# Second mixer's values with high and low parts in one stationary tile, four buffers in the norms, last modulation sums moved to a norm

## What is computed

```python
def hybrid_mixer(h, w_in, b_f, g_q, g_k, w_o):
    proj = h @ w_in
    ...
    sb_out = stick_breaking_attention(split_heads(sb_q, N_SB_HEADS), ...)
    fq = rms_norm(split_heads(fox_q, N_FOX_HEADS), g_q[None, :, None, :])
    fk = rms_norm(split_heads(fox_k, N_FOX_HEADS), g_k[None, :, None, :])
    ...
    fox_out = forgetting_attention(fq, fk, split_heads(fox_v, N_FOX_HEADS), log_f_cum)
    heads = jnp.concatenate([sb_out, fox_out], axis=1)
    return heads.transpose(0, 2, 1, 3).reshape(b, s, MIX_WIDTH) @ w_o

def second_block(x, c, ...):
    c_act = jax.nn.silu(c)
    mod = c_act @ w_mod[l] + b_mod[l]
    sh1, sc1, ga1, sh2, sc2, ga2, sh3, sc3, ga3 = jnp.split(mod, N_MOD, axis=-1)
    h = modulate(rms_norm(x, g_ffn1[l]), sh1, sc1)
    x = x + 0.5 * (1 + ga1[:, None, :]) * swiglu(h, ...)
    h = modulate(rms_norm(x, g_mix[l]), sh2, sc2)
    x = x + (1 + ga2[:, None, :]) * hybrid_mixer(h, ...)
    h = modulate(rms_norm(x, g_ffn2[l]), sh3, sc3)
    x = x + 0.5 * (1 + ga3[:, None, :]) * swiglu(h, ...)
```

## Time and profile before

| | us |
|---|---|
| median of 3 runs | 1822.4 (1821.92 to 1823.87) |
| the profiled execution | 1822.21 |
| its span, first to last instruction | 1820.5 |
| PE busy | 1805.6 (99%) |
| PEld busy | 1500.7 (82%) |
| DVE busy | 974.6 (54%) |
| ACT busy | 663.7 (36%) |
| POOL busy | 30.7 (2%) |

### The profile page before, as it was taken

The page is one execution under the profiler, slowest core; times in us unless marked ns, Lnnn a source line. Parts: engine busy times, 40 slices in busy tenths (PEclk is TensorE's granted clock), DMA queues, the critical chain, the costliest instruction groups (busy, mean ns, idle before and its releaser), DMA issues. The chain is left out here.

```text
span 1820.5 us, 20752 instructions
## 1 busy us (share of the span) xinstructions
PE 1805.6 (99%) x8593; PEld 1500.7 (82%) x8593; DVE 974.6 (54%) x1349; ACT 663.7 (36%) x1020; POOL 30.7 (2%) x62
## 2 busy tenths in 40 slices
PE   9999999999999999999999999999999999999998
PEld 8888888887888888878888888888888888888887
DVE  5655453457777766674433333666757543333332
ACT  5544441334323323352222222564656432122222
POOL 0000000000000000000000000010100000000001
PEclk9999999999999999999999999999999999999999
DMA  5232233355586565233333332322121333333333
GB/s 151 74 88 82 81 87 90 90 184 172 188 257 228 186 199 193 82 94 103 93 91 94 94 103 84 91 58 58 47 58 36 93 93 101 96 93 104 93 90 96
DMA packets 321859, 200.02 MB, mean 110 GB/s; under 512 B 6712, under 2 KB 311270, under 8 KB 321766
## 3 DMA queue, kind: packets, MB, share of 16 engines
q1 hardware_dynamic: 320882, 196.31, 35.9%
q0 software_dynamic: 640, 2.10, 0.4%
q10 hardware_dynamic: 244, 0.30, 0.1%
HBM read 196.58 MB, written 2.10 MB: 109 GB/s over the span
## 5 line engine op out<-in xcount | busy, mean ns | idle before, releaser
L1466 PE MATMUL ps<-u_hi,w_hi 128*128 128x512 f32 (+1 forms) x1704 | 667.1, 391 | 3.3 <-ACT u_hi L471 1.1
L1466 PE MATMUL ps<-u_hi,w_lo 128*128 128x512 f32 (+1 forms) x1704 | 660.2, 387 | 0.0
L1466 PE MATMUL ps<-u_lo,w_hi 128*128 128x512 f32 (+1 forms) x1704 | 655.4, 388 | 0.0
L885 DVE TENSOR_TENSOR w_lo<-w_raw,w_hi 128x1024 fp32r<-128x1024 f32 (+2 forms) x307 | 364.3, 1187 | 269.6 <-ACT w_hi L451 268.6
L451 ACT ACTIVATE w_hi<-w_raw 128x1024 fp32r<-128x1024 f32 (+2 forms) x307 | 314.5, 1025 | 239.0 <-DMA w_raw<-in_w_down 79.7
L1466 PEld LDWEIGHTS ps<-u_hi,w_hi 128*128 128x128 f32 x1704 | 320.0, 188 | 71.7 <-issue 4.3
L1466 PEld LDWEIGHTS ps<-u_hi,w_lo 128*128 128x128 f32 x1704 | 319.9, 188 | 66.2
L1466 PEld LDWEIGHTS ps<-u_lo,w_hi 128*128 128x128 f32 x1704 | 318.8, 188 | 67.2 <-DVE u_lo L919 2.9
L1466 PE MATMUL ps<-y_hi,w_hi 128*128 128x512 f32 x656 | 256.0, 390 | 0.0
L1466 PE MATMUL ps<-y_hi,w_lo 128*128 128x512 f32 x656 | 255.3, 389 | 0.0
L1466 PE MATMUL ps<-y_lo,w_hi 128*128 128x512 f32 x656 | 255.2, 389 | 0.0
(11 more groups left out here) (279 smaller groups left out, 1299.8 us busy)
## 6 DMA issues: line engine op xcount, KB each, us to landing
mod_raw<-in_w_mod SPq DMA_DIRECT2D x72, 512.0 KB, 4.8
w_raw<-in_w_in SPq DMA_DIRECT2D x71, 512.0 KB, 3.9
w_raw<-in_w_ffn_up SPq DMA_DIRECT2D x44, 512.0 KB, 4.0
w_raw<-in_w_gate SPq DMA_DIRECT2D x44, 512.0 KB, 3.8
w_raw<-in_w_up SPq DMA_DIRECT2D x44, 512.0 KB, 3.8
w_raw<-in_w_down SPq DMA_DIRECT2D x32, 512.0 KB, 3.9
w_raw<-in_w_ffn_down SPq DMA_DIRECT2D x16, 512.0 KB, 4.1
w_raw<-in_w_down SPq DMA_DIRECT2D x16, 384.0 KB, 3.4
```

Of the source, the lines that this page charges most:

```text
L885: e.tensor_tensor(w_lo[u % SLOTS][:, 0:n_k, :], w_raw[u % SLOTS][:, 0:n_k, :], f32(w_hi[u % SLOTS][:, 0:n_k, :]), ALU.subtract).then_inc(l ...
L1466: return e.matmul(out_, lhsT, rhs, start=start, stop=stop, skip_group_check=skip)
```

## The change

**Values.** In the second mixer the low parts of the values go into the half of `v_hi` that held zeros: the tile of head `n` is its high part in its own 64 columns and its low part in the other 64. Two matmuls (with the high and with the low part of the probabilities) replace three; the result has high x (high + low) in the head's own rows of PSUM and low x (high + low) in the other rows. The heads can therefore no longer share a bank: the second head of a step writes the projection bank from which the next step's keys were taken (`value_bank`), and waits until it is read. ACT copies the low half across to the head's own rows of `pair_out` (`take_low`), DVE adds the high half (`add_high`). `at_out` now comes with the first head's sum and a new semaphore `second_out` with the second's; PE waits for `second_out` behind the scores of the next step, ahead of its first strip. The pairs 6 and 7 are summed in `t_b` and then cut like the others, pair 6 ahead of 4 and 5. POOL's two memsets go.

**Norms.** Four buffers instead of two (`t_b[0]`, `t_a[0]`, `t_b[1]`, `t_a[1]`), so that chunk `c` waits for the low part of chunk `c - 4`. In ffn1, DVE waits for `plain_total` one chunk later, and ACT waits for six low parts before it writes the root of the first block's last norm into `t_a[0]`.

**Modulation.** Group 2 has 24 tiles, group 3 has 16. Group 3 is turned by PE behind the sums of norm mix2, in the place of 12 of 18 filler matmuls, and reduced by DVE behind that norm.

```diff
-MOD_GROUPS = ((0, 20), (20, 32), (32, 52), (52, 72))
+MOD_GROUPS = ((0, 20), (20, 32), (32, 56), (56, 72))
...
+        def scaled_tile(c):
+            return (t_b[c // 2 % 2][:, :], t_a[c // 2 % 2][:, 2:2 + SEQ])[c % 2]
+        def own_rows(n):
+            return slice(HEAD_DIM * n, HEAD_DIM * (n + 1))
+        def value_bank(i, n):
+            if n == 0:
+                return bank(slot_banks(i, 0)[0])
+            return ubank(U["proj"] + 3 * i + 4) if i + 1 < N_STEPS else bank(slot_banks(i, 0)[2])
+        def pair_out(i):
+            return heads[:, i, :] if i < N_STEPS - 2 else t_b[i - (N_STEPS - 2)][:, :]
...
+            def take_low(i):
+                for n in range(2):
+                    e.wait_ge(at_valued, 2 * i + n + 1)
+                    e.activation(pair_out(i)[own_rows(n)], value_bank(i, n)[own_rows(1 - n)], ACT.Copy).then_inc(low_out, 1)
             def fill_head(c):
-                e.activation(u_hi[:, c, :], heads[:, c, :], ACT.Copy).then_inc(u_hi_set, 1)
+                e.wait_ge(second_out, c + 1)
+                e.activation(u_hi[:, c, :], pair_out(c), ACT.Copy).then_inc(u_hi_set, 1)
...
-                for c in range(2, KC):
-                    e.wait_ge(u_lo_set, f * KC + c - 1)
+                scaled(2)
+                low(1).then_inc(u_lo_set, 1)
+                for c in range(3, KC):
+                    if c >= 4:
+                        e.wait_ge(u_lo_set, f * KC + c - 3)
                     scaled(c)
                     low(c - 1).then_inc(u_lo_set, 1)
...
-                    ins = e.tensor_tensor(v_lo[:, :, h, cols], ubank(u)..., f32(v_hi[:, :, h, cols]), ALU.subtract)
+                    ins = e.tensor_tensor(v_hi[:, :, h, own_rows(1 - h)], ubank(u)..., f32(v_hi[:, :, h, cols]), ALU.subtract)
...
+            def add_high(i):
+                for n in range(2):
+                    e.wait_ge(low_out, 2 * i + n + 1)
+                    out_ = pair_out(i)[own_rows(n)]
+                    e.tensor_tensor(out_, value_bank(i, n)[own_rows(n)], out_, ALU.add).then_inc((at_out, second_out)[n], 1)
...
             total("mix2")
-            keep_busy(18)
+            mod_turn(3)
+            keep_busy(6, 0)
...
+                if n and i + 1 < N_STEPS:
+                    u_k = p0 + 3 * i + 4
+                    e.wait_ge(bank_read[u_k % 2], u_k // 2 + 1)
...
-                    ins = three(ps[:, slot_banks(i, 0)[0], j * P:SEQ], (v_hi[:, j, n, :], v_lo[:, j, n, :]), (p_hi[n][:, at], p_lo[n][:, at]),
-                                n == 0 and j == 0, True, skip=True)
+                    for pp in (p_hi[n], p_lo[n]):
+                        ins = mm(value_bank(i, n)[:, j * P:], v_hi[:, j, n, :], pp[:, at], j == 0 and pp is p_hi[n], True, skip=True)
...
                 (sb_scores if i < N_SB else fox_scores)(i)
+                if i:
+                    e.wait_ge(second_out, i)
```

More of the change, by code:

```diff
@@ L470, in norm @@
                     e.wait_ge(normed, n0 + h + 1)
-                    ins = e.activation(u_hi[:, 0, half(h)], t_b[0][:, half(h)], ACT.Identity, bias=shift(0))
+                    ins = e.activation(u_hi[:, 0, half(h)], scaled_tile(0)[:, half(h)], ACT.Identity, bias=shift(0))
                     ins.then_inc(first_half_hi if h == 0 else u_hi_set, 1)
@@ L474, in norm @@
                     e.wait_ge(normed, n0 + c + 2)
-                    e.activation(u_hi[:, c, :], t_b[c % 2][:, :], ACT.Identity, bias=shift(c)).then_inc(u_hi_set, 1)
+                    e.activation(u_hi[:, c, :], scaled_tile(c), ACT.Identity, bias=shift(c)).then_inc(u_hi_set, 1)
             def residual(u0, which=None):
@@ L672, in scalar @@
             e.wait_ge(plain_total, 1)
+            e.wait_ge(u_lo_set, FILL["ffn1"] * KC + 6)
             after_own(e.activation(plain_r, bank(5), ACT.Ln, bias=EPS_COL[EPS1], scale=1.0 / D_MODEL))
@@ L781, in scalar @@
             take_v(0)
-            e.wait_ge(pool_set, 10)
+            e.wait_ge(mod_turned, sum(MOD_BANKS))
             stage_v(0)
@@ L812, in scalar @@
                     stage_normed(0)
-                e.wait_ge(at_valued, 2 * i + 2)
-                e.activation(heads[:, i, :], bank(slot_banks(i, 0)[0]), ACT.Copy).then_inc(at_out, 1)
+                take_low(i)
                 stage_v(i + 1)
@@ L831, in scalar @@
                     cut_hi(u + 3)
-                    e.wait_ge(at_valued, 2 * i + 2)
-                    e.activation(u_hi[:, i, :], bank(slot_banks(i, 0)[0]), ACT.Copy).then_inc(u_hi_set, 1)
+                    take_low(i)
+                    fill_head(i)
                     break
@@ L846, in scalar @@
                         fill_head(c)
-                e.wait_ge(at_valued, 2 * i + 2)
-                if i + 2 == N_STEPS:
-                    e.activation(u_hi[:, i, :], bank(slot_banks(i, 0)[0]), ACT.Copy).then_inc(u_hi_set, 1)
-                else:
-                    e.activation(heads[:, i, :], bank(slot_banks(i, 0)[0]), ACT.Copy).then_inc(at_out, 1)
+                take_low(i)
                 stage_v(i + 1)
                 if i + 2 == N_STEPS:
-                    for c in HEAD_ORDER[5:7]:
+                    for c in HEAD_ORDER[4:7]:
                         fill_head(c)
@@ L928, in norm @@
                     scaled(0, half(h))
-                if which == "ffn1":
-                    e.wait_ge(plain_total, 1)
                 scaled(1)
@@ L1252, in vector @@
             norm("mix2", U["gate_f"])
+            for k in range(MOD_BANKS[3]):
+                mod_sum(3, k)
+            mod_finish(3)
             p0 = U["proj"]
@@ L1340, in fill_head @@
                 e.wait_ge(u_hi_set, FILL["heads"] * KC + pos + 1)
-                e.tensor_tensor(u_lo[:, c, :], heads[:, c, :], f32(u_hi[:, c, :]), ALU.subtract).then_inc(u_lo_set, 1)
+                e.tensor_tensor(u_lo[:, c, :], pair_out(c), f32(u_hi[:, c, :]), ALU.subtract).then_inc(u_lo_set, 1)
             cut_lo(p0 + 2)
@@ L1380, in vector @@
                     stage_normed(i + 1)
+                add_high(i)
                 stage_v(i + 1)
@@ L1395, in vector @@
                     cut_lo(u + 3)
-                    e.wait_ge(u_hi_set, FILL["heads"] * KC + KC)
-                    e.tensor_tensor(u_lo[:, i, :], bank(slot_banks(i, 0)[0]), f32(u_hi[:, i, :]), ALU.subtract).then_inc(u_lo_set, 1)
+                    add_high(i)
+                    fill_head(KC - 1)
                     break
@@ L1407, in vector @@
                         fill_head(pos)
-                    e.wait_ge(u_hi_set, FILL["heads"] * KC + 5)
-                    e.tensor_tensor(u_lo[:, i, :], bank(slot_banks(i, 0)[0]), f32(u_hi[:, i, :]), ALU.subtract).then_inc(u_lo_set, 1)
+                add_high(i)
                 stage_v(i + 1)
                 if i + 2 == N_STEPS:
-                    for pos in range(5, 7):
+                    for pos in range(4, 7):
                         fill_head(pos)
@@ L1424, in gpsimd @@
             e.memset(t_a[1][:, 0:2], 0.0).then_inc(pool_set, 1)
-            for t in (v_hi, v_lo):
-                e.memset(f32(t[:]), 0.0).then_inc(pool_set, 1)
-            e.wait_ge(mod_turned, sum(MOD_BANKS))
             for t in (v_hi, v_lo):
@@ L1712, in ffn @@
                         unit(U[f, "down", part] + c, y_act, (y_lo_set, Y_FILL[f, part]) if c == 0 else None)
-                    if f == 1 and part == 0:
-                        mod_turn(3)
             def mod_turn(g):
```

22 lines of the change are left out of this document (9 added, 13 removed).

## The result

| | before | after |
|---|---|---|
| median of 4 runs, us | 1822.27 (1821.92 to 1823.87) | 1813.04 (1811.28 to 1814.50) |
| the profiled execution, us | 1822.21 | 1811.28 |
| its span, us | 1820.5 | 1809.6 |
| granted clock of the four runs after | | 1.000, 0.998, 0.997, 0.998 |

The ratio of the medians' runs is 0.9946, with a 95% interval of 0.9935 to 0.9958: the kernel is faster by 9.2 us. The forecast was 1811.9 us, the range 1809.0 to 1816.0. The profiled pair differs by 10.9 us, more than the medians do. That gap of 1.7 us became the open question of this study.

What follows compares the result with a forecast made beforehand. PE, busy 99% of the span, was taken to bound the kernel. Attention 7.5, modulation 1.7 and norms 1.25 sum to 10.5 us off 1822.2, giving 1811.7, or 1811.9 us for the median; range 1809.0 to 1816.0.

Steps and rivals of the forecast that it cites:

- The values, steps 0 to 5: Second mixer: fewer matmuls save 1.28 us a step, with no PE wait for the sums; 7.7 us in all.
- T+4.1: T is the start of a step's values; the second head's sum was to be ready 4.1 us later.
- Step 6: ACT and DVE also cut finished heads there: its 1.28 us is lost and 0.95 us more, allowed 0.6 to 1.3.
- Step 7: The second head's low parts hold PE 0.33 and 0.13 us; 0.8 us of the 1.28 us stay.
- Modulation: The block of 20 transposes goes and another block gets four more: 1.7 us saved, added DVE work costed at nothing.
- Norms: DVE's chunks lose the wait for the instruction right ahead: 1.25 us saved over four norms, bounds 0 and 1.9.
- the longer wait at the first turn of step 7: PE's wait for the probabilities at step 7's first turn was to be about 2.2 us instead of 0.60.
- slower: Rival: copy into other partitions and sum cost over 3.5 times their 1.28 us; total passes 1822.4 us; chance 0.04.

Runs made afterwards that it cites:

- d1: The changed kernel with each ACT copy of a half done twice and each DVE sum preceded by another operation of its size: lowest 1815.81, median 1817.28 us.
- e1: The kernel before with the values part of the change alone: lowest 1814.38, median 1817.64 us, ratio 0.9969.
- e3: The kernel before with the modulation part of the change alone: lowest 1820.10, median 1820.96 us, ratio 0.9989.
- n1: The changed kernel with the wait for the low part just ahead put back at each norm chunk, four buffers kept: lowest 1812.70, median 1814.41 us.
- r1: The changed kernel again, unaltered, five runs beside the kernel before: lowest 1814.24, median 1814.62 us, ratio 0.9954.
- g1: The kernel before with three tile copies on DVE ahead of step 7's first division, lengthening PE's wait: median 1823.20 us, ratio 1.0005.
- g2: The kernel before with two pauses, three DVE copies ahead of pair 6's low part and two ahead of step 7's first division: median 1825.32 us.
- g3: The kernel before with seven tile copies on DVE ahead of step 7's first division: lowest 1826.16, median 1827.58 us, ratio 1.0025.
- e2: The kernel before with the norms part of the change alone: lowest 1820.38, median 1820.71 us, ratio 0.9990.
- f1: The changed kernel with ACT and DVE work reordered at the end of step 6 and in step 7: lowest 1809.68, median 1811.75 us.

## Why the prediction was right

**The values, steps 0 to 5**: forecast 1.28 us each, measured 1.27 to 1.32. The copy was taken as 0.60 us and is 0.59, the sum 0.68 and is 0.69, and the second sum is ready at T+3.99 where T+4.1 was worked out. d1 shows the cover of about 1 us, and e1's profile has 7.7 us for the whole part, forecast 7.5.

**Step 6**: forecast a wait of 0.85 us at the last scores, 2.2 us at the first turn and a net loss of 0.95 (0.6 to 1.3); the profile after has 0.72, 1.93 and 0.99. (The prediction's own terms, 0.60 + 0.95 + 0.43, give 1.98 and not 2.2 for the wait at the turn.) DVE's timeline there, the sums and the staging of the next values:

```profile
1381.76 1.40 DVE L1304 TENSOR_TENSOR t_b<-ps,t_b 64x512 f32<-64x512 f32 x2
1383.19 0.76 DVE L1297 TENSOR_TENSOR v_hi<-ps,v_hi 128x256 fp32r<-128x256 f32 x2
```

The two sums take 1.40 us together, 2 x 0.69, and the staging starts 0.03 us behind their end. Nothing overlaps here, where the partitions change, as the Trainium skill has it (VectorE: DVE Perf Modes, "Two Vector instructions with no wait between them"). In the kernel before, DVE's instruction behind L1409, which reads PSUM and lasts 0.68 us as the sums do, starts 0.60 us after it, before its end:

```profile
1392.83 0.74 DVE L1273 TENSOR_TENSOR v_lo<-ps,v_hi 128x256 fp32r<-128x256 f32 x2
```

Against that, 0.71 us from sum to sum is about 0.1 us more for each of the two, the 0.2 us that the prediction gave. That it is the partitions that hold them, no run parts from other causes.

**Step 7**: forecast 0.8 of 1.28 us, measured 0.75, with a wait of 0.28 us at the second head's values (forecast 0.33).

**Modulation**: forecast 1.7, by the trace 2.1 less 0.4, and e3 gives 1.3 by the lowest runs, 1.8 by the medians and 1.7 by its profile. No strip behind norm mix2 waited for a cut, so the DVE work there (forecast 3.2 us, 3.0 by DVE's timeline) was hidden. PE's wait for `u_hi` behind the fillers, 0.41 us before, is below 0.1 us now: the 16 turns and six fillers fill the cover nearly to its end, where the prediction still had PE waiting a little.

**Norms**: forecast 0.46, 0.46, 0.23 and 0.1; measured 0.42 (mix2, 9.57 us where it was 9.99), 0.48 (ffn2), 0.23 (ffn1) and about 0.1 (ffn0). n1 shows that the wait is the cause.

**The term that was mis-sized** is the longer wait at the first turn of step 7. The prediction priced it at its length, about 2 us where it was 0.60, and that was right for the profiled execution, which ran at full clock. In three of the six profiled executions with a wait of 1.7 to 2.0 us the clock falls behind it, and in r1 and e1 that costs 1.6 us more. The changed kernel's mean is 2.8 us over its lowest run, the kernel before's 1.5 (72 runs beside the experiments: lowest 1821.42, mean 1822.95). So of 10.1 us between the lowest runs 8.9 are left between the means. Half of 1.6 us is 0.8 of the 1.3 us between the 2.8 and the 1.5; where the rest is lost no profile shows. The falls at 1182 us don't explain it: they are in three of the eight profiles with the denser values and in three of the six without. The forecast of 1811.9 is the time at full clock; the medians were 1813.0 and, in the second series, 1814.6, inside the range, but nearer to its upper end than the sum says. As far as the traces go, the sum's error lies there and nowhere else: at full clock the pair's 10.4 us stand against 10.5. The prediction's remark that the runs lie within 0.1% of each other was too narrow as well, both kernels spread over 0.3%.

One rival was summed wrongly. For "slower" the prediction has over 2.1 us lost in each of seven steps and passes 1822.4 only there; 7 x 2.1 us on 1811.9 are 1827, and 1822.4 is passed at about three times the cost of copy and sum. With copy and sum at 0.59 and 0.69 us nothing hangs on it.

The last wait of a residual for `x`, 0.42 us in the trace of the kernel before, is 0.2 to 0.3 us in the profiles of g1, g2 and g3, which change nothing at that place: it varies from run to run and is no gain of the change.

## What to carry to other kernels

A full-width partner for a half-empty stationary tile paid here wherever the adding of the halves had cover, 1.3 us a step. Count the cover step by step; here the last two steps, where other work had been stacked, were the ones without it. Price a pause of TensorE above its length where the traces show the clock falling behind such pauses (here 3 of 6 of 1.7 to 2.0 us, both of over 3 us), and look at the granted clock of several runs, not only at the profiled one. In these norms an instruction on VectorE that waited for the one just ahead cost 0.12 us each time; two more buffers took that away.

## What the runs showed of the hardware that I had not expected

- PE's clock fell to half behind a wait of 1.9 us in some executions and within a wait of 3.5 us in the one profiled, at its lower level for 3.4 or 6.8 us. In steps 6 and 7 it was not seen to fall behind waits of up to 1.2 us. But in e1 it was at half for 6.8 us also in step 3, from 1288.7 us, behind two waits of 0.73 and 0.59 us that the kernel before has as well: 1 of 14 profiles.
- It also fell for 3.4 us in six of fourteen profiles (r1, e2, f1, d1, g2, g3) between 1182 and 1189 us, behind a stretch where PE is busy without a pause, but with matmuls of 8 columns and transposes: 1.5 us a time. That the narrow work is the cause is not shown; a fuller stretch there wasn't tried.
- Every one of the fourteen profiles also ends with 0.6 to 3.5 us at half clock, which moves the granted clock of the whole run by up to 0.001: a difference of that size between single runs says nothing.
- A copy on ACT and a sum on DVE over 64 partitions cost what those over 128 do (0.59 and 0.69 us at 512 columns), and the copy takes no longer for moving its 64 rows to the other half of the partitions on the way.
